# Block attention turned by VectorE and by transfers in place of TensorE

## What is computed

```python
s = jnp.einsum('bqhd,bqkhd->bhqk', qb.astype(jnp.float32), k_sel.astype(jnp.float32)) * (HEAD_DIM ** -0.5)
s = jnp.where(valid[:, None], s, -jnp.inf)
p = jax.nn.softmax(s, axis=-1)
return jnp.einsum('bhqk,bqkhd->bqhd', p.astype(v.dtype), v_sel)
```

## Time and profile before

| | us |
|---|---|
| median of 3 runs | 1549.55 (1548.9 to 1550.58) |
| profiled execution, time | 1550.08 |
| profiled execution, span | 1547.9 |
| attention's units in the profile | 295 to 424.3 |
| from the slot behind the last filler matmul to the second total | 424.3 to 444.0 |
| granted TensorE clock, mean share of full speed | 0.998 |

### The profile page before, as it was taken

The page is one execution under the profiler, slowest core; times in us unless marked ns, Lnnn a source line. Parts: engine busy times, 40 slices in busy tenths (PEclk is TensorE's granted clock), DMA queues, the critical chain, the costliest instruction groups (busy, mean ns, idle before and its releaser), DMA issues.

```text
span 1547.9 us, 20637 instructions
## 1 busy us (share of the span) xinstructions
PE 1519.1 (98%) x7186; PEld 1252.6 (81%) x7186; DVE 1129.6 (73%) x1849; ACT 744.6 (48%) x1259; POOL 654.1 (42%) x291
## 2 busy tenths in 40 slices
PE   9999999999999999999999999999999999999998
PEld 7888888777888877888888888777779887888887
DVE  6689999887775445776777759776744887677775
ACT  6553233344462345754444245554763745444444
POOL 3444444322334432144555545351543344555551
PEclk9999999999999999999999999999999999999999
DMA  5333333212143323333333123222002432333321
GB/s 210 100 123 97 100 96 95 82 55 69 55 148 96 95 82 109 108 97 97 97 109 104 53 94 97 82 82 68 26 31 87 145 115 90 97 106 109 96 95 55
DMA packets 40419, 145.26 MB, mean 94 GB/s; under 512 B 4484, under 2 KB 4612, under 8 KB 40072
## 3 DMA queue, kind: packets, MB, share of 16 engines
q1 hardware_dynamic: 39312, 140.47, 28.4%
q10 hardware_dynamic: 1016, 3.61, 0.7%
HBM read 141.95 MB, written 2.11 MB: 93 GB/s over the span
## 4 chain that ended last, share of the span: by engine, by line
PE 87%; DVE 5%; issue 3%; ACT 3%; POOL 1%; DMA 1%; SPq 0%; DVEq 0%; ACTq 0%; POOLq 0%
PE bank L656 85%; PE bank L766 1%; DMA w_raw<-in_stream 1%; DVE x_sq L2176 0%; DVE cq_rstd L2112 0%; PE bank L1214 0%; DVE bias L2258 0%; ACT w_hi L1437 0%; POOL w_lo L530 0%; POOL dn_rest L540 0%; POOL res L625 0%; DMA dn_raw<-in_stream 0%; ACT kT L1611 0%; PE bank L1387 0%; PE bank L1030 0%
## 5 line engine op out<-in xcount | busy, mean ns | idle before, releaser
L530 POOL TENSOR_TENSOR w_lo<-w_raw,w_hi 128x1024 fp32r<-128x1024 f32 x191 | 473.3, 2490 | 524.9 <-ACT w_hi L1437 524.6
L656 PE MATMUL bank<-a_hi,w_hi 128*128 128x512 f32 (+1 forms) x1120 | 445.4, 398 | 2.6 <-DVE a_lo L3040 1.8
L656 PE MATMUL bank<-a_hi,w_lo 128*128 128x512 f32 (+1 forms) x1120 | 432.1, 386 | 0.0
L656 PE MATMUL bank<-a_lo,w_hi 128*128 128x512 f32 (+1 forms) x1120 | 431.7, 385 | 0.0
L1437 ACT CAST w_hi<-w_raw 128x1024 fp32r<-128x1024 f32 x199 | 204.9, 1048 | 177.5 <-DMA w_raw<-in_stream 177.4
L656 PEld LDWEIGHTS bank<-a_hi,w_hi 128*128 128x128 f32 x1120 | 210.7, 188 | 49.5 <-issue 3.8
L656 PEld LDWEIGHTS bank<-a_lo,w_hi 128*128 128x128 f32 x1120 | 210.7, 188 | 45.3 <-issue 3.3
L656 PEld LDWEIGHTS bank<-a_hi,w_lo 128*128 128x128 f32 x1120 | 210.7, 188 | 42.5
L540 POOL TENSOR_TENSOR dn_rest<-dn_raw,dn_first 128x1024 fp32r<-128x1024 f32 x13 | 31.4, 2416 | 276.2 <-DVE f_lo L2562 276.2
L656 PE MATMUL bank<-dn_rest,f_hi 128*128 128x512 f32 x364 | 141.6, 389 | 0.0
L1707 ACT CAST dn_first<-dn_raw 128x1024 fp32r<-128x1024 f32 x54 | 55.7, 1048 | 167.1 <-DVE dn_raw L2495 167.1
(11 more groups left out here) (427 smaller groups left out, 2880.3 us busy)
## 6 DMA issues: line engine op xcount, KB each, us to landing
w_raw<-in_stream SPq DMA_DIRECT2D x199, 512.0 KB, 3.5
dn_raw<-in_stream SPq DMA_DIRECT2D x56, 512.0 KB, 3.6
res<-in_xT ACTq DMA_DIRECT2D x1, 2048.0 KB, 8.0
out_y<-res_tok SPq DMA_DIRECT2D x8, 256.0 KB, 2.0
x_raw<-in_xT SPq DMA_DIRECT2D x3, 512.0 KB, 8.3
mem_raw<-in_memT SPq DMA_DIRECT2D x1, 1024.0 KB, 11.8
mrow<-m_rows ACTq DMA_DIRECT2D x4, 256.0 KB, 3.1
w_raw<-in_stream SPq DMA_DIRECT2D x2, 256.0 KB, 3.7
```

Source lines behind the costliest of these rows:

```text
L530: nc.gpsimd.tensor_tensor(w_lo[:, j, :], w_raw[:, j, :], w_hi[:, j, :].bitcast(F32), ALU.subtract).then_inc(w_lo_done, 1)
L656: return nc.tensor.matmul(o, l, r, start=start, stop=stop)
```

## The change

TensorE no longer turns the probabilities. They are turned in three steps. VectorE turns each square of 32x32 by itself (`dsa_turn`), which leaves the squares of a 128x128 block in their old places across the partitions, in `d_parts`, one buffer that holds a whole head (4 x 10 x 32 columns, 640 KB). SyncE stores it to device memory (`p_parts`) and reads it back by four loads of 32 partitions each, in pieces of 1280 bytes, into `d_turned`, also one buffer (`turn_parts`). TensorE multiplies a whole head with the values (`dsa_values`, 10 matmuls), four units later than the head's last: after the filler of unit 4G + 7, for the last head in the middle of the projection. The first turn of a head waits until the store of the head before has landed; the loads wait for the values of the head before.

The scaling by the reciprocal moves from VectorE to ScalarE (`dsa_scaled`), the copies out of the bank are gone, and the scores have four banks instead of two. ScalarE rounds head G in unit 4G + 8 and the last head between the squares of the layer norm, and issues the load of `res` after the squares. The semaphores are counted anew in the other attentions; nothing else changes there.

```diff
+            def turn_parts(G):
+                sp.wait_ge(sems["pT_ready"], 4 * G + 4)
+                sp.dma_start(p_parts[G], d_parts[:, :, :, :].rearrange("p g k j -> p (g k j)")).then_inc(sems["p_stored"], 16)
+                sp.wait_ge(sems["p_stored"], 16 * (G + 1))
+                if G > 0:
+                    sp.wait_ge(sems["pv_done"], 4 * G)
+                rows = p_parts[G].rearrange("(g i) (h n) -> h i g n", g=RING, h=RING)
+                for h in range(RING):
+                    sp.dma_start(d_turned[PART * h:PART * h + PART, :, :, :].rearrange("i g k j -> i g (k j)"), rows[h]
+                                 ).then_inc(sems["p_landed"], 16)
+
+            for G in range(HEADS):
+                turn_parts(G)
+                ring(first + 2 * G + 1)
+                ring(first + 2 * G + 2)
...
-            attend(DSA_G, HEADS, dsa_score,
-                   lambda G, kb: values[:, kb, G * P:(G + 1) * P], dsa_hook)
+
+            def dsa_scores(n):
+                G, qb = n // 4, n % 4
+                if n >= RING:
+                    pe.wait_ge(sems["p_ready"], n - RING + 1)
+                dsa_score(G, qb, ps[4 + n % RING][:, 0:(qb + 1) * P]).then_inc(sems["s_ready"], 1)
+
+            def dsa_values(G):
+                pe.wait_ge(sems["p_landed"], 16 * RING * (G + 1))
+                if G > 0:
+                    pe.wait_ge(sems["o_ready"], G)
+                for qb in range(TB):
+                    for kb in range(qb + 1):
+                        m = mm(ps[2][:, qb * P:(qb + 1) * P].rearrange("p (g j) -> p g j", g=RING),
+                               values[:, kb, G * P:(G + 1) * P], d_turned[:, :, part_of(qb, kb), :], kb == 0, kb == qb)
+                    m.then_inc(sems["pv_done"], 1)
...
+            for n in range(4 * HEADS):
+                if n + 2 < 4 * HEADS:
+                    dsa_scores(n + 2)
+                dsa_hook(n)
+                if n % 4 == 3 and n >= 7:
+                    dsa_values(n // 4 - 1)
...
+            pe.wait_ge(sems["p_ready"], 4 * HEADS)
             ln_total(1)
...
+            ao_chunk(0, range(HEADS - 1))
+            dsa_values(HEADS - 1)
+            ao_chunk(1, range(HEADS - 1))
+            ao_chunk(0, range(HEADS - 1, HEADS))
+            ao_chunk(1, range(HEADS - 1, HEADS))
+            for j in range(2, KB):
+                ao_chunk(j, range(KB))
                 if j == LN_VAR_AFTER:
                     ln_total(2)
...
+            def dsa_exps(n):
+                act.wait_ge(sems["s_masked"], n + 1)
+                if n >= 2:
+                    act.wait_ge(sems["pT_ready"], n - 1)
...
+            def dsa_scaled(n):
+                act.wait_ge(sems["p_inv"], n + 1)
+                p = d_probs[n % 2][:, 0:(n % 4 + 1) * P]
+                A.activation(p, p, ACT.Copy, scale=rowinv[:, n % 2:n % 2 + 1]).then_inc(sems["p_scaled"], 1)
...
+            dsa_exps(0)
+            for n in range(4 * HEADS):
+                dsa_scaled(n)
+                if n + 1 < 4 * HEADS:
+                    dsa_exps(n + 1)
+                dsa_hook(n)
+                if n % 4 == 0 and n >= 8:
+                    head_hi(n // 4 - 2)
+            head_hi(HEADS - 2)
...
                 if k == 4:
+                    head_hi(HEADS - 1)
                     round_to(CH["AO"] + 1)
+            act.dma_start(res[:, :, :], xT).then_inc(x_again, 16)
...
+            def dsa_turn(n):
+                G, qb = n // 4, n % 4
+                dve.wait_ge(sems["p_scaled"], n + 1)
+                if G > 0 and qb == 0:
+                    dve.wait_ge(sems["p_stored"], 16 * G)
+                V.transpose(d_parts[:, :, part_of(qb, 0):part_of(qb, qb) + 1, :].rearrange("p g k j -> p k g j"),
+                            d_probs[n % 2][:, 0:(qb + 1) * P].rearrange("p (k g i) -> p k g i", g=RING, i=PART)
+                            ).then_inc(sems["pT_ready"], 1)
...
+            for n in range(4 * HEADS):
+                dsa_inverse(n)
+                if n >= 1:
+                    dsa_turn(n - 1)
+                if n % 4 == 1 and n >= 9:
+                    out_lo(n // 4 - 2)
+                if n + 2 < 4 * HEADS:
+                    dsa_mask(n + 2)
+                dsa_hook(n)
+            dsa_turn(4 * HEADS - 1)
+            out_lo(HEADS - 2)
```

More of the change, by code:

```diff
@@ L101, with part_of @@
 RING = 4
+PART = 32
+TRIANGLE = 10
+def part_of(qb, kb):
+    return qb * (qb + 1) // 2 + kb
 AHEAD = 3
@@ L266, in program @@
         spread = at("spread", [P, TB, P], TMP0 + 8192)
+        d_probs = [at(f"d_probs{i}", [P, T], C0 + 14336 + 16384 * i) for i in range(2)]
+        d_parts = at("d_parts", [P, RING, TRIANGLE, PART], TMP0 + 2048)
+        d_turned = at("d_turned", [P, RING, TRIANGLE, PART], TMP0 + 7168)
         x_raw = at("x_raw", [P, KB, T], G0)
@@ L481, in left, with rings @@
                                  ).then_inc(dn_landed[LEFT.index(name)], 16)
[L483 to L488 removed]
+            def rings(first, last):
+                with sp.Fori(first // RING, last // RING) as i:
+                    for j in range(RING):
+                        sp.wait_ge(chunk_done, RING * i + j - (RING - 1))
+                        sp.dma_start(w_raw[:, j, :],
+                                     stream[bass.ds(RING * i + j, 1), :, :].rearrange("o p n -> (o p) n")
+                                     ).then_inc(raw_landed[j], 16)
+            def turn_parts(G):
[8 more added lines that the diff above has]
+                                 ).then_inc(sems["p_landed"], 16)
+            first = CH["ATT"] + 8
+            rings(RING, first // RING * RING)
+            for c in range(first // RING * RING, first + 1):
+                ring(c)
+            for G in range(HEADS):
+                turn_parts(G)
+                ring(first + 2 * G + 1)
+                ring(first + 2 * G + 2)
+            then = first + 2 * HEADS + 1
+            for c in range(then, (then + RING - 1) // RING * RING):
+                ring(c)
+            rings((then + RING - 1) // RING * RING, CH["FF1"] // RING * RING)
             for c in range(CH["FF1"] // RING * RING, CH["FF1"]):
```

63 lines of the change are left out of this document (39 added, 24 removed).

## The result

The changed kernel takes 1556.6 us (median of 5 runs, 1555.44 to 1558.87), the kernel before 1549.8 us beside it (1548.9 to 1550.58). The ratio is 1.0047, with a 95% interval of 1.0033 to 1.0062: slower by about 7 us, where no change was forecast.

The account below looks back on a forecast made before the run. TensorE, busy for 98% of the 1547.9 us span, was taken as the bound. The loop's -7.3 us and the tail's +7.4 summed to +0.1: 1549.7 us against a median of 1549.55, range 1545.5 to 1557.

Parts of the forecast that it names:

- Removed: Block attention loop: 80 turns leave TensorE (8.8 us); with the kT wait uncovered, a head takes about 16.5 us, 0.66 saved.
- Start: Start of the loop: the score of unit 8, which waits for kT, starts at 313.5 for 315.63, 2.1 us early.
- The turn: VectorE's turn by 32x32 squares, priced like the mask's steps: 0.21, 0.34, 0.48, 0.60 us, 1.63 a head, covered.
- T: The slot behind the loop's last filler matmul, forecast at 417.0 us in place of 424.33.
- rival D: Values matmuls cost more because they stream pieces of 32 columns; half of +12.8 us is +6.4, 1556; chance 0.05.
- rival A: Slow store, VectorE waits for d_parts at a head's first turn; decides beyond 6.2 us; 8.3 us gives 1568; chance 0.13.
- rival B: VectorE's turn costs much more than one pass: 1552.6 at twice the value, 1567 like a reciprocal; chance 0.12.
- rival C: Quicker transfers: store 3.5 us, last load 2.0 to 2.4, landing about T + 8.0; 1547.7, down to 1546; chance 0.25.
- values of head 7 (2.2): Tail: TensorE's values matmuls for the last head, behind the wait for its landing, take 2.2 us.
- 5.6 us from that cast to the end of the last addition: Tail: from ScalarE's cast of chunk 4's weight to the end of the layer norm's last addition, 5.6 us as before.
- 7.4 us were to be given back: Tail: the second total starts at T + 27.0 in place of T + 19.6, losing 7.4 us.
- landing of head 7: Tail: the last head's store (4.8 us) and loads (last 3.1 us) land at T + 10.0, a TensorE wait of 2.1 us.

Follow-up runs that it names:

- E3: The changed kernel with 13 matmuls without use before the values of head 7 and 21 before the second total: 1557.68 us, ratio 1.0041.
- E6: The changed kernel run once more with nothing altered: 1560.29 us (a single run).
- E7: The changed kernel with ScalarE's cast of projection chunk 5 moved behind the square root: 1555.9 us, ratio 1.0037.
- E1: The changed kernel with ScalarE's cast of projection chunk 4 moved behind all eight squares: 1552.31 us, ratio 1.0009.
- E12: The changed kernel with eight waits for a semaphore long reached added to VectorE's program: 1555.58 us, ratio 1.0038.
- E5: The kernel before, run once more with nothing altered: 1550.47 us, ratio 1.0003.
- the two edits: On the changed kernel: chunk 4's cast behind all squares, and head 7's values behind seven steps of chunk 1 too; together 1549.42 us, ratio 0.9993.
- the third: Added to the two edits: two steps of projection chunk 2 ahead of the eighth steps of chunks 0 and 1; all three 1546.55 us, ratio 0.9972.
- E2: The changed kernel with the values of head 7 behind seven steps of projection chunk 1 too: 1556.52 us, ratio 1.0035.

## Why the prediction was wrong

**The loop was right, and a little cautious.** From the mask to the slot behind the last filler it took 120.3 us for 129.2, 8.9 us less, against 7.3 forecast. Removed: as said (head 16.45 us, 16.5 forecast). Start: the lone store took 2.9 us and not 4.0 (issued 306.98, first load 309.87), so turn(4) waited for nobody, and the first score that waits for kT came 3.4 us earlier, counted from the first mask, and not 2.1. The profile of the result was also a lucky one: five of the ten profiles with the changed loop lose 1.6 us of the 8.9 again to a fall of the clock behind the wait for kT, which no step of the prediction has.

**The turn.** 0.31, 0.43, 0.56, 0.69 us against my 0.21, 0.34, 0.48, 0.60: dearer, and covered. Values in pieces cost 0.11 us an instruction (20 in 2.23 us, in all seven blocks up to T): rival D was out. The typical store took 5.3 us, 5.8 at most: rival A was out, as its point of 6.2 us was not reached. With the turn of 128x512 at 0.69 us, rival B was out. The Trainium skill (DMA: Bandwidth & Descriptors, section Anatomy of one DMA) gives the formula behind rival C for transfers that GpSimd issues, and these are SyncE's. In place of its estimated 3.5 us the store took 2.9 alone and 5.3 among the weight loads, so C's quicker landing did not come.

**The tail was wrong, in the steps "values of head 7 (2.2)" and "5.6 us from that cast to the end of the last addition".** The path was named rightly (two waits, for the landing and for the additions, through chunk 0, the weight of chunk 4 and its cast), and 7.4 us were to be given back; from T to the second total it gave back 12.1 (31.7 us for 19.6). By step, counted from T:

| step | forecast | measured |
|---|---|---|
| landing of head 7 | T + 10.0 | T + 10.85 |
| values of head 7 | 2.2 | 3.9 |
| chunk 0 complete, its slot loaded | T + 17.7 | T + 20.5 |
| load and wait until the cast of chunk 4 | 3.6 | 3.6 |
| cast to the end of the last addition | 5.6 | 7.6 |
| second total | T + 27.0 | T + 31.7 |
| extra behind the second total | 0 | 1.7 |

Two sizes were taken from the trace of before as if they held in the new place. The 0.11 us of a values instruction is the price at the upper clock; I put it behind a wait that I had myself forecast, and TensorE came out of that wait at the lower one. E3 shows it: no standing, no fall, 2.3 us. It is not certain in every execution: of five profiles with that wait unfilled (2.6 to 3.0 us), three came back at the lower clock (3.5 to 3.9 us for the values: changed, E6, E7) and two did not (2.25: E1, E12). And the 5.6 us of the earlier trace rows (the two times are 5.7 apart) hold a single remainder on GpSimd beside the additions. In the new tail ScalarE casts chunk 4 so late that chunk 5 has landed too: it casts both, and the second remainder falls on the additions (E7, and E1 with none). The third term, the clock behind the second wait (1.7 us), was in no step. The landing, a smaller miss of 0.85 us, came late because turn(31) ended at T + 0.7 and not at T + 0.2, and the store took 5.3 us and not 4.8.

**The sum, then**: +0.1 forecast; -1.6 from the loop, +4.7 in the tail, +1.7 behind it: +4.9 up to kxT, which is what the marks show. The range's upper part spoke of a slow store; the loss came from elsewhere.

**Nobody forecast the last 3 us.** "Nothing else changes there" was true of the code and not of the time. By the traces 1.6 us of it are the one negm_diag instruction (E1 against E5). The rest, about 1.2 us between kxT and kh, is not settled: the old loop's four profiles have 461.8 to 462.3 us there, the changed loop's ten 461.8 to 463.4. A late fall that costs 1.6 us stands in both profiles (1109 us before, 1161 changed) and takes no part in the difference.

## What to carry to other kernels

When a step waits for a transfer, its price is not only the wait: ask at which clock TensorE may come back, and which late casts and remainders now fall together behind it. Take away all the waits of one path and look for the next one behind them: here the two edits gave 5.9 and 1.9 us by the ratios, 8.4 together, and only the third, which filled a new wait of 1.40 us, brought the kernel below the one before. The gain of a loop is only kept if the drain behind it is filled with independent work: with three edits of order this change is worth 0.28%, and without them it costs 0.47%. And a gain or loss of 1 to 2 us in 1550 is read from marks in the traces; the medians of five runs on different chips do not carry it.

## What the hardware showed that was not expected

- TensorE stood 2.8 us and came back at 0.56 of the clock in the next 3 us. Such a fall does not follow every wait: behind the wait of 2.0 us at 311 us it came in five of ten profiles of the same loop, behind the waits of 2.6 to 3.0 us before the values of head 7 in three of five, behind those of 3.1 to 5.2 us before the second total in five of five (changed, E2, E6, E7, E12). Most falls cost 1.2 to 1.7 us (2.1 behind E2's wait of 5.15 us, 2.9 behind E7's of 3.13), and 0.1 at most at 1078 to 1094 us.
- Three VectorE additions with two inputs in the on-chip memory: 2.27 us alone, 4.03 beside one GpSimd subtraction of 128x1024, 5.99 beside two; a single VectorE instruction of 0.28 us took 2.45 beside one. In each case one instruction pays, the one that starts while the subtraction runs; one that started 0.15 us ahead of it paid nothing.
- A 640 KB store to device memory took 2.9 us, until its first load was issued, with no weight load beside it (heads 0 and 6); the median of the eight, with weight loads among them, was 5.3, the longest 5.8.
- Eight waits of no meaning in VectorE's program took away a gap of 0.19 us 600 us further on, and with it 1.6 us of one stretch, in both profiles that have them.
